# The second key's squared distance made on ScalarE, token by token, in place of a subtraction on Pool

## The chip, the cores and the metric

The kernel runs on one core of a Trainium2 chip. The metric is the time of one execution in microseconds on the device. A core has TensorE (matmuls; its weight loads are a line of their own in the profile), VectorE, ScalarE, Pool and the SyncE queue that issues DMAs. Each runs its own list of instructions in order, and they wait for one another by counting semaphores.

## The reference

One inference step of a decoder trunk of two layers, for 256 prompt tokens and 32 sample tokens (288 columns in all). Each layer is a mixer followed by a PEER channel mixer, which is where the change lies:

```python
def block(hb):
    q = (hb @ wq).reshape(T, PEER_HEADS, 2, PEER_DK // 2)
    s = jnp.einsum('thpc,hpkc->thpk', q, keys)
    v1, i1 = lax.top_k(s[:, :, 0], PEER_TOPK)
    v2, i2 = lax.top_k(s[:, :, 1], PEER_TOPK)
    comb = (v1[..., :, None] + v2[..., None, :]).reshape(T, PEER_HEADS, PEER_TOPK * PEER_TOPK)
    vals, sel = lax.top_k(comb, PEER_TOPK)
    e1 = jnp.take_along_axis(i1, sel // PEER_TOPK, axis=-1)
    e2 = jnp.take_along_axis(i2, sel % PEER_TOPK, axis=-1)
    eid = e1 * N_KEYS + e2
    gate = jax.nn.softmax(vals, axis=-1)
    act = jax.nn.gelu(jnp.einsum('thkd,td->thk', u[eid], hb), approximate=False)
    w = (gate * act).astype(hb.dtype)
    return jnp.einsum('thk,thkd->td', w, v[eid])
```

Each token has 8 heads with 16 picks each, so 128 picks, and each pick is a pair of keys (e1, e2) out of 128 x 128 experts.

## The kernel before

All 128 x 128 experts are computed for all tokens. In stage `u` of a layer TensorE multiplies the tokens with all of `peer_u`, and ScalarE writes the Gelu of it (L517) to `gates`, one column of 128 second keys for each first key and token. In stage `v` the weighted `gates` are multiplied with `peer_v`. The weights from Gelu to weighted `gates` are made in between, in the **gate loop**, which the change edits: for each token TensorE multiplies a 128 x 128 one-hot of the first key, scaled by the softmax gate, with a 128 x 128 one-hot of the second key, and the product (first key by second key) is multiplied into `gates`.

The gate loop has 12 iterations (`T // TOKENS`, 24 tokens each), and each iteration has six groups of four tokens (index `g`). The tile `choice` holds, with one row for each pick and one column for each token, the first key, the second key and the gate. It is filled by `turn_picks` on VectorE at the end of stage `u`. In each group:

- Pool (L367) writes into `apart` the distance of every second key from the picked one: `iota` (0 to 127 along the row) less the key, for four tokens in one instruction of 128x512.
- ScalarE squares `apart` (L528), and after its own semaphore makes 1 - square, cut off at 0, into `seconds` (L531, a Relu): this is the second one-hot.
- VectorE makes the first one-hots with four instructions of 128x128 (`firsts`, L1090).
- TensorE multiplies the two, token by token (L1409; a product of float32 is two matmuls in the profile), into PSUM.
- VectorE multiplies the 128x512 product into `gates` (`apply`, L1096). Its order is firsts of group 0, then for each group the firsts of it and the apply of the group before, and the last apply at the end of the iteration.

`apart` and `seconds` hold two groups, `onehot` eight tokens, PSUM two groups; `onehot_free`, `gate_free` and `second_ready` count them. Pool may write `apart` once the Relu two groups before is through.

In the first layer the gate loop carries the conditioning of the second layer as well. An iteration begins on TensorE with 16 matmuls of `condition` (L1212). ScalarE copies the result out in two halves (`next_row`, L470, after the Relu of groups 0 and 2), TensorE transposes each half after groups 1 and 3 (`turn`, L1239), and ScalarE adds the bias to the transposed columns (`next_column`, L477, two instructions each, after the Relu of groups 2 and 4).

Pool's list has, besides, the spill of x ahead of the gate loop and its reload, which waits for the first expert output of stage `v`.

Of the kernel before, what the change touches and what calls it, by code (L numbers as in the profile page):

```python
# [24 lines left out]
F32 = mybir.dt.float32  # L25
F32R = mybir.dt.float32r
U32 = mybir.dt.uint32
ALU = mybir.AluOpType
ACT = mybir.ActivationFunctionType
AX = mybir.AxisListType  # L30

P = 128
# [5 lines left out]
T = T_PROMPT + T_SAMPLE  # L38
# [63 lines left out]
def trunk(nc, t):  # L102

    with ExitStack() as ctx:
# [3 lines left out]
        def sem(name):  # L108
            return ctx.enter_context(nc.semaphore(name))
# [151 lines left out]
        exped, picks_ready = sem("exped"), sem("picks_ready")  # L261
        first_ready, second_ready = sem("first_ready"), sem("second_ready")
        onehot_free = sem("onehot_free")
        apart_ready, apart_squared = sem("apart_ready"), sem("apart_squared")
        gate_free = sem("gate_free")
        gelu_ready, topk_done, choice_ready, w_ready = sem("gelu_ready"), sem("topk_done"), sem("choice_ready"), sem("w_ready")
        w_high, w_low = sem("w_high"), sem("w_low")
# [74 lines left out]
        @block.gpsimd  # L342
        def _(pool):
            pool.dma_start(cs[:], t["c"]).then_inc(c_landed, 16)
            pool.dma_start(x, t["x"]).then_inc(x_landed, 16)
            for dst, src in ((ones[:], t["ones"]), (ident[:], t["ident"]), (iota[:], t["iota"]),
                             (ada_b[:], t["ada_b"]), (norm_g[:], t["norm_g"]), (small[:, 32:64], t["gains"])):
                pool.dma_start(dst, src).then_inc(const_landed, 16)
            for dst, src in ((cos_t, t["cos"]), (sin_t, t["sin"]), (swap, t["swap"]), (q_decay, t["q_decay"]),
                             (att_decay, t["att_decay"]), (att_decay_s[0:T_SAMPLE], t["att_decay_s"]),  # L350
                             (key_decay, t["key_decay"]), (seq_mask[0:T_SAMPLE], t["seq_mask"]),
                             (ret_state, t["state_ret"]), (conv_zs[:, :, :, 0:2], t["state_conv"])):
                pool.dma_start(dst, src).then_inc(ret_tables, 16)

            def peer(l):
                pool.wait_ge(mixer_done, l + 1)
                pool.dma_start(keys, t["peer_keys"][l]).then_inc(keys_landed, 16)
                pool.wait_ge(x_ready, 2 * l + 1)
                pool.dma_start(x_spill, x).then_inc(x_spilled, 16)

                pool.wait_ge(choice_ready, l + 1)
                pool.wait_ge(gelu_ready, EXP * (l + 1))
                with pool.Fori(0, T // TOKENS) as i:
                    for g in range(TOKENS // 4):
                        n = i * (TOKENS // 4) + (T // 4 * l + g)
                        pool.wait_ge(second_ready, n + 1)
                        pool.tensor_tensor(apart[:, g % 2], iota[:, None, :].broadcast_to([P, 4, P]),  # L367
                                           choice[:, 1, bass.ds(i * TOKENS + 4 * g, 4)][:, :, None].broadcast_to([P, 4, P]),
                                           ALU.subtract).then_inc(apart_ready, 1)
                pool.wait_ge(half_done, 2 * (SPLIT[f"v{l}"] + KC + 1))  # L370
                pool.dma_start(x, x_spill).then_inc(x_back, 16)


            pool.wait_ge(state_ready, 1)
            pool.dma_start(t["ret_p"], ret_s2).then_inc(state_stored, 16)
            pool.dma_start(t["ret_s"], ret_state).then_inc(state_stored, 16)
            pool.dma_start(t["conv_p"], conv_tail).then_inc(state_stored, 16)
            pool.dma_start(t["conv_s"], conv_tails).then_inc(state_stored, 16)
            peer(0)
            pool.wait_ge(half_done, 2 * (SPLIT["v0"] + EXP))  # L380
            for dst, src in ((restart, t["restart"]), (lev_mask, t["lev_mask"]), (lev_masks[0:T_SAMPLE], t["lev_masks"]),
                             (h_seq_mask[0:T_SAMPLE], t["seq_mask"]), (bounds, t["bounds"])):
                pool.dma_start(dst, src).then_inc(hg_tables, 16)

            def load_state(head, slot):
                pool.dma_start(s_in[:, slot:slot + 1], t["state_hgrn"][:, bass.ds(of_head(head, 1, 0), 1)]).then_inc(s_landed[slot], 16)

            def store_state(head, slot):
                pool.wait_ge(s_updated, of_head(head, 1, 1))
                pool.dma_start(t["hg_s"][:, bass.ds(of_head(head, 1, 0), 1)], s_out[:, slot:slot + 1]).then_inc(s_stored[slot], 16)  # L390
            for j in range(2):
                load_state((0, j), j)
            with pool.Fori(0, HG_HEADS // 2 - 1) as pair:
                for j in range(2):
                    store_state((pair, j), j)
                    pool.wait_ge(s_stored[j], pair * 16 + 16)
                    load_state((pair + 1, j), j)
            for j in range(2):
                store_state((HG_HEADS // 2 - 1, j), j)
            for j in range(2):  # L400
                pool.wait_ge(s_stored[j], 16 * (HG_HEADS // 2))
            pool.wait_ge(state_ready, 2)
            pool.dma_start(t["hg_p"], h_out).then_inc(state_stored, 16)
            peer(1)
            for half in range(2):
                chunks = slice(4 * half, 4 * half + 4)
                pool.wait_ge(y_ready, half + 1)
                pool.dma_start(t["y"][:, chunks], h[:, chunks]).then_inc(out_done, 16)
            pool.wait_ge(out_done, 32)
            pool.wait_ge(state_stored, 16 * 5)  # L410
            pool.wait_ge(x_spilled, 32)
# [3 lines left out]
        def _(act):  # L415
# [93 lines left out]
            def peer(l):  # L509
                norm(2 * l + 1)  # L510
                high_input(3 * l + 3)
                act.wait_ge(state_stored, 64 if l == 0 else 80)
                copy_out(f"wq{l}", query, ACT.Copy, (0, WQ // 4))
                act.wait_ge(x_spilled, 16 * (l + 1))

                def expert_in(i, s):
                    act.activation(gates[:, bass.ds(i * 4 + s, 1), :], ps[:, s % 2:s % 2 + 1, 0:T], ACT.Gelu).then_inc(gelu_ready, 1)  # L517
                read_out(f"u{l}", expert_in, groups=(0, topk_row // 4))
                act.wait_ge(topk_done, l + 1)
                act.activation(rstd[:], rstd[:], ACT.Exp).then_inc(exped, 1)  # L520
                read_out(f"u{l}", expert_in, groups=(topk_row // 4, EXP // 4))
                if l == 0:
                    act.sem_inc(second_ready, 2)
                with act.Fori(0, T // TOKENS) as i:
                    for g in range(TOKENS // 4):
                        n = i * (TOKENS // 4) + (T // 4 * l + g)
                        act.wait_ge(apart_ready, n + 1)
                        act.activation(apart[:, g % 2], apart[:, g % 2].bitcast(F32), ACT.Square).then_inc(apart_squared, 1)  # L528
                        act.wait_ge(apart_squared, n + 1)
                        act.wait_ge(onehot_free, i * TOKENS + (T * l + 4 * g + 4))  # L530
                        act.activation(seconds[:, g % 2], apart[:, g % 2].bitcast(F32), ACT.Relu, bias=1.0, scale=-1.0).then_inc(second_ready, 1)  # L531
                        if l == 0:
                            if g in (2, 4):
                                next_column(i + 12, g // 2 - 1, i * 4)
                            if g in (0, 2):
                                next_row(i + 12, g // 2)
                if l == 0:
                    high(SPLIT["v0"], FIRST["v0"] // 4, 0)

                def weight_high(e, slot):  # L540
                    act.activation(hs[:, 0, bass.ds(slot, 1), :], gates[:, bass.ds(e, 1), :], ACT.Copy).then_inc(w_high, 1)  # L541

                act.wait_ge(w_ready, (T // 4) * (l + 1))
                weight_high(0, 0)

                def expert_out(i, s):
                    split_high(f"v{l}", i, s)
                    if not (isinstance(i, int) and 4 * i + s == EXP - 1):
                        act.wait_ge(half_done, i * 8 + 2 * (SPLIT[f"v{l}"] + s))
                        weight_high(i * 4 + (s + 1), (s + 1) % 2)  # L550
                section(act, f"v{l}", expert_out)
# [83 lines left out]
        def _(dve):  # L635
# [15 lines left out]
            def released():  # L651

                dve.wait_ge(glue_free, taken.at())
# [414 lines left out]
            def turn_picks(l):  # L1068
# [6 lines left out]
                    ins = dve.transpose(choice[:, q, T_PROMPT:T], pick_of[2][:, q, :])  # L1075
                link(ins)
                released()
                dve.sem_inc(choice_ready, 1)

            def weigh(l):  # L1080
# [479 lines left out]
```

## Time and profile before

| | |
|---|---|
| median of 3 runs | 2921.69 us (2921.49 to 2928.01) |
| span of the profiled execution | 2932.5 us |
| TensorE busy | 2684.2 us (92%) |
| VectorE busy | 1793.5 us (61%) |
| ScalarE busy | 1351.1 us (46%) |
| Pool busy | 181.9 us (6%) |

The profile is one execution on the chip, and its times run from the first to the last instruction. A busy time is an average over stages with different limits, so each stage is read by itself. The granted clock is the share of full speed that TensorE's clock has in a stretch: 1.0 is 2.4 GHz and 0.5 is 1.2 GHz. In a timeline a row may merge several instructions of one line; the bracket behind it says how long the engine stood idle before and what it waited for.

### The profile page before, as it was taken

What the parts mean: (1) busy time and instruction counts of PE and PEld (TensorE: products, weight loads), DVE (VectorE), ACT (ScalarE), POOL (GpSimd) and SP (SyncE); (2) the same over time, 40 slices, a digit from 0 to 9 for tenths busy, and PEclk for the clock granted to TensorE, in tenths of its full rate; (3) what the DMA queues carried; (4) which work ended last, traced back from release to release, by engine and by line L of the source; (5) the groups of instructions that cost most, each with busy time, mean ns of one, the idle gap of its engine ahead of it and who ended that gap; (6) DMA issues with size and microseconds to landing.
All of it is one profiled execution on the core that took longest, in us unless ns stands there. A gap on an engine that the chain in (4) does not pass through costs nothing.

```text
span 2932.5 us, 55686 instructions
## 1 busy us (share of the span) xinstructions
PE 2684.2 (92%) x17972; PEld 2441.2 (83%) x17972; DVE 1793.5 (61%) x4076; ACT 1351.1 (46%) x2491; POOL 181.9 (6%) x200
## 2 busy tenths in 40 slices
PE   7997899999989899999979796999999866999997
PEld 3962799999955579999979685899999855999996
DVE  2424568884466755555554877589854599555554
ACT  2501345556543445555545323355556544455553
POOL 1000000000022310000000000000000144000000
PEclk8987899999998989999989788899999978999998
DMA  6544444545533335555534112345445300555552
GB/s 231 165 130 161 132 137 158 168 148 163 162 124 100 100 127 182 164 165 164 165 120 162 37 57 102 122 151 161 154 158 165 122 0 0 167 165 165 165 165 86
DMA packets 108380, 401.03 MB, mean 137 GB/s; under 512 B 12352, under 2 KB 12496, under 8 KB 107168
## 3 DMA queue, kind: packets, MB, share of 16 engines
q1 hardware_dynamic: 103104, 375.44, 39.7%
q0 software_dynamic: 5216, 24.87, 2.3%
q8 instruction: 29, 0.48, 0.1%
q14 instruction: 31, 0.25, 0.0%
HBM read 389.60 MB, written 10.65 MB: 136 GB/s over the span
## 4 chain that ended last, share of the span: by engine, by line
PE 81%; DVE 12%; issue 3%; ACT 2%; DMA 1%; DVEq 1%; ACTq 0%; POOL 0%; SPq 0%; POOLq 0%
PE ps L1184 21%; PE ps L1186 21%; PE ps L1185 21%; PE ps L1212 6%; PE ps L1409 4%; DVE onehot L1090 2%; DVE spl L660 1%; PE ps L1329 1%; PE ps L1345 1%; DVE big L1096 1%; PE ps L1358 1%; DMA raw<-in_ada_w 1%; PE ps L1248 1%; DVE big L1041 1%; DVE big L1036 1%
## 5 line engine op out<-in xcount | busy, mean ns | idle before, releaser
L1184 PE MATMUL ps<-hs,spl 128*128 128x288 f32 x4960 | 1481.8, 299 | 75.9 <-DVE hs L712 46.0
L1185 PE MATMUL ps<-hs,spl 128*128 128x288 f32 x4960 | 1473.0, 297 | 0.0
L1186 PE MATMUL ps<-hs,spl 128*128 128x288 f32 x4960 | 1470.5, 296 | 0.0
L660 DVE TENSOR_TENSOR spl<-raw,spl 128x512 fp32r<-128x512 f32 x1240 | 844.4, 692 | 844.9 <-ACT spl L422 842.6
L422 ACT ACTIVATE spl<-raw 128x512 fp32r<-128x512 f32 x1240 | 774.4, 631 | 628.6 <-PE ps L1186 628.2
L1184 PEld LDWEIGHTS ps<-hs,spl 128*128 128x128 f32 x4960 | 940.1, 190 | 89.5 <-issue 58.2
L1186 PEld LDWEIGHTS ps<-hs,spl 128*128 128x128 f32 x4960 | 943.0, 190 | 0.0
L1185 PEld LDWEIGHTS ps<-hs,spl 128*128 128x128 f32 x4960 | 941.7, 190 | 0.0
L1409 PE MATMUL ps<-hs,onehot 128*128 128x128 f32 x1152 | 222.7, 346 | 81.0 <-DVE onehot L1090 56.5
L1409 PEld LDWEIGHTS ps<-hs,onehot 128*128 128x128 f32 x1152 | 185.0, 239 | 121.3 <-issue 56.8
L1090 DVE TENSOR_SCALAR onehot<-iota,choice 128x128 f32<-128x128 f32 x576 | 239.2, 480 | 5.5 <-PEq L1398 4.4
L367 POOL TENSOR_TENSOR hs<-iota,choice 128x512 fp32r<-128x512 f32 x144 | 152.3, 1058 | 1245.7 <-ACT big L517 1002.5
L1212 PE MATMUL ps<-raw,cs 128*10 128x512 f32 x384 | 184.5, 636 | 13.6 <-ACT cs L554 6.7
L517 ACT ACTIVATE big<-ps 128x288 f32 (+1 forms) x256 | 105.6, 412 | 177.9 <-PE ps L1186 177.2
L1212 PEld LDWEIGHTS ps<-raw,cs 128*10 128x10 f32 x384 | 34.7, 96 | 147.2 <-issue 128.5
L1096 DVE TENSOR_TENSOR big<-big,ps 128x512 f32 x144 | 98.0, 681 | 86.7 <-PE ps L1409 85.7
L531 ACT ACTIVATE hs<-hs 128x512 fp32r<-128x512 f32 x144 | 91.0, 632 | 86.6 <-PE ps L1409 78.0
L1123 DVE TENSOR_TENSOR hs<-big,hs 128x288 fp32r<-128x288 f32 x256 | 115.8, 452 | 0.6 <-ACT hs L541 0.6
L541 ACT ACTIVATE hs<-big 128x288 fp32r (+1 forms) x256 | 109.9, 429 | 5.5 <-DVEq L1104 5.5
L517 ACT ACT_TABLE_LOAD x62 | 79.5, 1283 | 63.1 <-PE ps L1186 63.1
L528 ACT ACTIVATE hs<-hs 128x512 fp32r<-128x512 f32 x144 | 88.7, 616 | 3.2 <-POOL hs L367 3.1
L484 ACT ACTIVATE big<-ps 128x288 f32 (+1 forms) x92 | 37.9, 412 | 95.8 <-PE ps L1186 95.7
(222 smaller groups left out, 1292.3 us busy)
## 6 DMA issues: line engine op xcount, KB each, us to landing
raw<-in_peer_u SPq DMA_DIRECT2D x256, 512.0 KB, 3.4
raw<-in_peer_v SPq DMA_DIRECT2D x256, 512.0 KB, 3.4
raw<-in_ada_w SPq DMA_DIRECT2D x96, 512.0 KB, 4.3
raw<-in_peer_wq SPq DMA_DIRECT2D x32, 512.0 KB, 3.3
raw<-in_hg_w_in SPq DMA_DIRECT2D x32, 512.0 KB, 3.4
raw<-in_ab_w_in SPq DMA_DIRECT2D x28, 512.0 KB, 3.4
raw<-in_ab_w_out SPq DMA_DIRECT2D x8, 512.0 KB, 3.9
big<-in_state_hgrn POOLq DMA_DIRECT2D x8, 512.0 KB, 3.9
```

What stands on the lines that cost most here:

```text
L367: pool.tensor_tensor(apart[:, g % 2], iota[:, None, :].broadcast_to([P, 4, P]), choice[:, 1, bass.ds(i * TOKENS + 4 * g, 4)][:, :, None].b ...
L422: act.activation(spl[:, slot % 2, 0, cols], raw[:, slot, cols], ACT.Copy).then_inc(high_ready, 1)
L517: act.activation(gates[:, bass.ds(i * 4 + s, 1), :], ps[:, s % 2:s % 2 + 1, 0:T], ACT.Gelu).then_inc(gelu_ready, 1)
L660: dve.tensor_tensor(spl[:, slot % 2, 1, cols], raw[:, slot, cols], spl[:, slot % 2, 0, cols].bitcast(F32), ALU.subtract).then_inc(low_read ...
L1090: dve.tensor_scalar(onehot[:, (4 * g + j) % 8, :], iota[:], choice[:, 0, bass.ds(tok, 1)], choice[:, 2, bass.ds(tok, 1)], ALU.is_equal, AL ...
L1096: dve.tensor_tensor(w, w, ps[:, 6 + g % 2, :].rearrange("p (j e) -> p e j", j=4), ALU.mult).then_inc(gate_free, 1)
L1123: dve.tensor_tensor(hs[:, 1, slot, :], gates[:, bass.ds(e, 1), :].rearrange("p a t -> p (a t)"), hs[:, 0, slot, :].bitcast(F32), ALU.subtr ...
L1184: pe.matmul(out, spl[:, slot, 0, cols], high, start=start, stop=False, skip_group_check=True)
L1185: pe.matmul(out, spl[:, slot, 0, cols], low, start=False, stop=False, skip_group_check=True)
L1186: return pe.matmul(out, spl[:, slot, 1, cols], high, start=False, stop=stop, skip_group_check=True)
L1212: ins = pe.matmul(out, cs[:, k, :], raw[:, k // 2, ROWS * (k % 2):ROWS * (k % 2) + ROWS], start=k == 0, stop=k == KC - 1)
L1409: pe.matmul(ps[:, 6 + g % 2, j * P:j * P + P], onehot[:, (4 * g + j) % 8, :], seconds[:, g % 2, j, :].bitcast(F32), start=True, stop=True) ...
```

## The change

The subtraction on Pool and its semaphore are gone. VectorE negates the second key in `choice` once, at the end of `turn_picks`. ScalarE makes the square by itself: four instructions of 128x128 for a group, each with `iota` as input and the token's column of the negated key as bias, and the last one of the four raises the semaphore that the Relu waits for. ScalarE now waits for `choice_ready` ahead of the loop, and for the Relu two groups before (its own) in place of Pool.

```diff
-                pool.wait_ge(choice_ready, l + 1)
-                pool.wait_ge(gelu_ready, EXP * (l + 1))
-                with pool.Fori(0, T // TOKENS) as i:
-                    for g in range(TOKENS // 4):
-                        n = i * (TOKENS // 4) + (T // 4 * l + g)
-                        pool.wait_ge(second_ready, n + 1)
-                        pool.tensor_tensor(apart[:, g % 2], iota[:, None, :].broadcast_to([P, 4, P]),
-                                           choice[:, 1, bass.ds(i * TOKENS + 4 * g, 4)][:, :, None].broadcast_to([P, 4, P]),
-                                           ALU.subtract).then_inc(apart_ready, 1)
...
+                act.wait_ge(choice_ready, l + 1)
                 with act.Fori(0, T // TOKENS) as i:
                     for g in range(TOKENS // 4):
                         n = i * (TOKENS // 4) + (T // 4 * l + g)
-                        act.wait_ge(apart_ready, n + 1)
-                        act.activation(apart[:, g % 2], apart[:, g % 2].bitcast(F32), ACT.Square).then_inc(apart_squared, 1)
+                        act.wait_ge(second_ready, n + 1)
+                        for j in range(4):
+                            ins = act.activation(apart[:, g % 2, j], iota[:], ACT.Square, bias=choice[:, 1, bass.ds(i * TOKENS + (4 * g + j), 1)])
+                        ins.then_inc(apart_squared, 1)
                         act.wait_ge(apart_squared, n + 1)
...
                 link(ins)
                 released()
+                link(dve.tensor_scalar(choice[:, 1, :], choice[:, 1, :], -1.0, None, ALU.mult))
                 dve.sem_inc(choice_ready, 1)
```

## Rows read from the trace of the kernel before

**Rows 1.** Stretch table: stretch, length, busy us (count), granted clock, DMA share, GB/s
```profile
824.40:1065.00 240.60, 212.78 (x864) 121.43 (x864) 159.06 (x360) 103.94 (x218) 75.42 (x72) 0.87 0.32 105
2325.90:2492.40 166.50, 112.92 (x576) 96.39 (x576) 161.24 (x360) 83.44 (x144) 76.92 (x72) 0.79 0.00 1
```

**Rows 2.** Source view of two lines: ns min/median/max, first and last start
```profile
L1090 DVE TENSOR_SCALAR onehot<-iota,choice x576: 332/340/1223, 824.5 to 2490.7; 128x128 f32<-128x128 f32 x192
L367 POOL TENSOR_TENSOR hs<-iota,choice x144: 1030/1041/1183, 824.5 to 2485.9; 128x512 fp32r<-128x512 f32 x144
```

**Rows 3.** Timeline of VectorE, both layers: start us, us, instructions [idle before]
```profile
2341.35 2.97 DVE L1090 TENSOR_SCALAR onehot<-iota,choice 128x128 f32<-128x128 f32 x8
...
925.69 2.14 DVE L1090 TENSOR_SCALAR onehot<-iota,choice 128x128 f32<-128x128 f32 x8
...
2488.32 1.11 DVE L1090 TENSOR_SCALAR onehot<-iota,choice 128x128 f32<-128x128 f32 x4
2489.34 0.68 DVE L1096 TENSOR_TENSOR big<-big,ps 128x512 f32 x1
2489.94 1.11 DVE L1090 TENSOR_SCALAR onehot<-iota,choice 128x128 f32<-128x128 f32 x4
```

**Rows 4.** Timeline of TensorE: groups at full and half clock, and a bubble
```profile
2488.79 1.18 PE L1409 MATMUL ps<-hs,onehot 128*128 128x128 f32 x8 [0.44 <-DVE onehot L1090]
...
842.58 2.02 PE L1409 MATMUL ps<-hs,onehot 128*128 128x128 f32 x8 [0.30 <-ACT hs L531]
...
2342.67 2.56 PE L1409 MATMUL ps<-hs,onehot 128*128 128x128 f32 x11 [2.10 <-DVE onehot L1090]
```

**Rows 5.** Timeline of ScalarE, start of the second layer's loop
```profile
2327.74 0.63 ACT L531 ACTIVATE hs<-hs 128x512 fp32r<-128x512 f32 x1
2328.27 0.61 ACT L528 ACTIVATE hs<-hs 128x512 fp32r<-128x512 f32 x1
2329.00 0.63 ACT L531 ACTIVATE hs<-hs 128x512 fp32r<-128x512 f32 x1
```

**Rows 6.** Groups of ScalarE by form: busy us, mean ns of one | idle before
```profile
L528 ACT ACTIVATE hs<-hs 128x512 fp32r<-128x512 f32 x144 | 88.7, 616 | 3.2 <-POOL hs L367 3.1
...
L594 ACT ACTIVATE big<-big 128x1280 f32<-128x1280 f32 x8 | 10.1, 1257 | 0.7 <-DVE big L880 0.7
...
L457 ACT ACTIVATE mod<-ps,ada_b 128x10 f32<-128x10 f32 x48 | 9.0, 272 | 22.9 <-PE ps L1231 22.7
L470 ACT ACTIVATE rstd<-ps 10x256 f32<-10x256 f32 x24 | 8.8, 366 | 96.2 <-PE ps L1212 96.2
```

**Rows 7.** Timeline of ScalarE: four instructions in a row, each with a bias tile
```profile
34.26 0.75 ACT L457 ACTIVATE mod<-ps,ada_b 128x10 f32<-128x10 f32 x4 [0.34 <-PE ps L1231]
```

**Rows 8.** Timelines of ScalarE and VectorE: ends of the second layer's loop
```profile
2325.08 0.41 ACT L517 ACTIVATE big<-ps 128x288 f32<-128x288 f32 x1 [2.27 <-PE ps L1186]
...
2325.89 5.13 DVE L1090 TENSOR_SCALAR onehot<-iota,choice 128x128 f32<-128x128 f32 x8 [1.11 <-ACT big L517]
...
2488.39 0.63 ACT L531 ACTIVATE hs<-hs 128x512 fp32r<-128x512 f32 x1 [0.42 <-PE ps L1409]
```

**Rows 9.** Timelines of TensorE and ScalarE: one iteration of the first layer's loop
```profile
913.91 1.16 PE L1409 MATMUL ps<-hs,onehot 128*128 128x128 f32 x8 [0.64 <-ACT hs L531]
...
917.89 0.94 PE L1409 MATMUL ps<-hs,onehot 128*128 128x128 f32 x6 [0.67 <-ACT hs L531]
919.23 0.57 PE L1409 MATMUL ps<-hs,onehot 128*128 128x128 f32 x2 [0.40 <-DVE onehot L1090]
919.73 1.02 PE L1239 MATMUL ps<-ident,rstd 10*128 10x10 f32 x4
...
924.87 7.74 PE L1212 MATMUL ps<-raw,cs 128*10 128x512 f32 x16
...
915.84 0.48 ACT L477 ACTIVATE mod<-ps,ada_b 128x10 f32 x2 [0.72 <-PE ps L1239]
...
920.98 0.56 ACT L477 ACTIVATE mod<-ps,ada_b 128x10 f32 x2 [1.89 <-PE ps L1239]
```

## What was predicted, and from what

> **What bounds the kernel now.** The change touches two stretches only, the gate loops of the two layers, so the first view is the stretch table, cut at their ends [rows 1]: 240.60 us in the first layer, 166.50 us in the second, of a span of 2932.5 us. Each is 12 iterations of six groups of four tokens, so 20.05 and 13.88 us an iteration. In the second layer VectorE is busy for 161.24 of 166.50 us: it is the bound. In the first layer TensorE is busy for 212.78 of 240.60 us, because each iteration also holds 16 conditioning matmuls (7.74 us in [rows 9]).
>
> Then the source view of the two lines that meet [rows 2]. A one-hot on VectorE (L1090) has a median of 340 ns and a maximum of 1223 ns; a subtraction on Pool (L367) has 1041 ns. The timeline shows what stretches the one-hots [rows 3]: eight of them take 2.97 us where a Pool subtraction runs beside them (2341.35) and 2.14 us where Pool is idle (925.69). After the last subtraction (it starts at 2485.9 [rows 2]) a group of four takes 1.11 us, and VectorE goes round once in 1.62 us (2488.32 to 2489.94). So one subtraction costs VectorE about 0.83 us, most of its own 1.04 us, and a round of the second layer, 13.88 / 6 = 2.31 us, is about 0.7 us longer than VectorE needs alone. I take this as exclusion between the two engines.
>
> TensorE needs 1.18 us for the 8 matmuls of a group at a granted clock of 1.0 and 2.02 us at 0.5 [rows 4]; the stretches' means are 0.87 and 0.79 [rows 1]. ScalarE has slack now: 83.44 of 166.50 us busy.
>
> **What goes.** The 144 subtractions leave Pool, and with them a semaphore hop from ScalarE to Pool and back. Nothing else on Pool moves: its reload of x still sits behind the wait for the expert output stage. What VectorE gets back is about 0.83 us a group, 60 us in each layer, of which only what no other engine needs becomes time.
>
> **What comes on ScalarE.** One Square of 128x512 becomes four of 128x128, each with a column of the choice tile as bias. Now a Square starts 0.53 us after the Relu before it, and the Relu 0.73 us after its Square [rows 5]: a round takes at least 1.27 us. For the small Square there is no row, so I bound it. Its length: 616 ns at 512 columns and 1257 at 1280 make 0.835 ns a column [rows 6], so 128 columns without a bias tile last 616 - 384 x 0.835 = 295 ns. The bias tile: L470 (256 columns, no bias tile) takes 366 ns, L457 (10 columns, with one) 272 ns [rows 6]; by columns the second should be 205 ns shorter and is 94 shorter, so the tile adds 0.11 us, and a small Square lasts 0.40 us. Its distance to the next: 0.53 - 384 x 0.000835 = 0.21 us if the tile costs nothing (lower bound); four L457 take 0.75 us [rows 7], so (0.75 - 0.27) / 3 = 0.16 us apart, and with 118 columns more 0.26; 0.32 if the tile's 0.11 is paid in full on top of 0.21; 0.40 if neighbours don't overlap (upper bound). I take 0.30, between the two middle values, as L457 reads PSUM and the Square reads SBUF. The address arithmetic of each Square runs on ScalarE's sequencer; I count it as hidden, and if it isn't, the upper bound is the case.
>
> The Trainium skill prices the same thing: "ScalarE: Activation LUTs", section "What ACT_TABLE_LOAD costs", says that a [128,1] pointer operand adds some 93 ns, that such an ACTIVATE takes about 280 ns + 0.833 ns a column, and that neighbours overlap by 93 ns. By that, as an estimate, a Square takes 387 ns at a distance of 294 ns, and the sum below would move by some 2 us.
>
> From the first Square to the Relu: 3 x 0.30 + 0.40 + 0.12 (0.73 less the Square's 0.616) = 1.42 us in place of 0.73. A round of ScalarE is then 1.42 + 0.53 = 1.95 us, above VectorE's free 1.62: **ScalarE becomes the bound of the second layer**.
>
> **Second layer.** The last Gelu starts at 2325.08 and lasts 0.41 [rows 8]. The Squares begin at 2325.5, the first Relu at 2326.9, the 72nd 71 x 1.95 = 138.5 us later, at 2465.4; before, it started at 2488.39 [rows 8]. That is 23 us less with TensorE at full clock. At half clock TensorE needs 2.02 us a group, and between iterations it stands still: VectorE applies the sixth group before it makes the next one-hots. This bubble is 2.10 us now [rows 4]; without Pool I reckon 0.7 (the apply of 2489.34 in [rows 3]) + 0.35 (first one-hot) + 0.1 = 1.15. So 6 x 2.02 + 1.15 = 13.3 us an iteration, and 12 x 0.58 = 7 us less than before is the poorest end. Groups of 8 matmuls every 1.62 us ran at full clock at the end of this loop [rows 4], and 1.95 us is not far from that: I take -22.
>
> **First layer.** Here three Squares stand in TensorE's way, for ScalarE is held by conditioning work in between. In an iteration [rows 9] the second group waits for its Relu (913.91), the fourth again (917.89) after L477 had waited for the first transposes (915.84), and the sixth's Square comes behind the second L477 (920.98). Each of the three becomes 0.69 us longer, so 2.1 us. Against that, the fourth group no longer waits for VectorE in its midst: its 8 matmuls would end 1.07 us after 917.89, the transposes behind them start at 919.73, so 0.8 us comes back. At the same clock an iteration is thus up to 1.3 us longer, and less where stretched one-hots, and not this chain, set its end now. If the clock falls one group earlier than now, the fourth group takes 2.02 in place of 1.1 us ahead of the chain: 2.3 us longer. I take 1.0 us, 12 us for the layer; ends 0 and +28.
>
> **Small edits.** The negation is one VectorE instruction on 128x288 (between 0.34 at 128 columns [rows 2] and 0.68 at 512 [rows 3]) and its wait, 0.5 us a layer. It lies in the 1.11 us that VectorE waits for the last Gelu in the second layer [rows 8], and beside the first conditioning matmuls in the first layer. If that cover were gone: 1 us in all. ScalarE's new wait for the choice holds up only the Squares behind it, and by then the choice is there. Both: 0, at most +1.
>
> **The sum**: -22 + 12 = -10 us. The profiled execution is given by its span, 2932.5 us; the runs have a median of 2921.69 (2921.49 to 2928.01), and 10 us scaled by their ratio stays 10. So 2911.7 us.
>
> **Rivals.**
> (a) *The clock pays it back.* TensorE's gaps grow in the first layer, and what falls to half clock makes the chain longer. Evidence: both loops already run at 0.87 and 0.79, not at 1.0. Price: -8 in the second layer, +28 in the first, so +20: 2942. It decides once most iterations of the first layer fall to half clock before the fourth group. The Trainium skill speaks for it: "TensorE: Matmul & The Clock Gate", section "HAM oscillation", says that idle stretches between bursts of matmuls bring the throttle back and that each burst then starts slow. The rows of half-clock groups agree that it happens here; whether more often after the change no row shows.
> (b) *Small Squares don't overlap* (0.40 apart): first Square to Relu 1.72, a round 2.25. Second layer 71 x 0.30 = 21 us worse, so about -1; first layer 3 x 0.3 x 12 = 11 worse, +23: slower by 22, 2944. Each 0.01 us of distance is worth some 3 us; the balance tips at 0.33. Against it: neighbours do overlap in [rows 5] and [rows 7].
> (c) *The bias tile is free* (0.21 apart, 0.30 long): a round 1.05 + 0.53 = 1.58, so VectorE's 1.62 bounds the second layer: 71 x 1.62 = 115 us, -46 at full clock, with bubbles and some half clock -33. First layer 0.3 less on each of three Squares, 0. About -33: 2889. Against it: the 0.11 us of [rows 6].
> (d) *The one-hots aren't stretched by Pool* but by something that stays: VectorE keeps its 13.88 us in the second layer, and in the first the fourth group still waits for it in part, so more than 12 us are paid there: +15, 2937. [Rows 3] speak against it.
>
> **Chances.** Forecast 0.45, (a) 0.22, (b) 0.15, (c) 0.13, (d) 0.05. The forecast's own range is 2897 to 2925. The range runs from (c) at its better half to (a): 2886 to 2943. A measurement here can tell about 0.3% (8.8 us) from no change. Faster by more: three quarters of the forecast and all of (c), 0.47. Within: the rest of the forecast and the milder part of (a) and (b), 0.27. Slower: 0.26.
>
> **What would show it.** L1090 at a mean near 340 ns in both layers; small Squares some 0.40 us long and 0.30 apart; the second layer's loop near 144 us with ScalarE busy for almost all of it and TensorE waiting for the Relu, no longer for one-hots; the first layer's loop near 252 us with longer waits of the second, fourth and sixth group for their Relus. Wrong if one-hots stay stretched, if Squares stand 0.35 us apart, or if the granted clock of either loop moves by more than 0.05.

## The result, and the profile after

The changed kernel takes 2929.99 us (median of 20 runs) where the one before took 2924.59 us beside it: a ratio of 1.0021, with a 95% interval of 1.0012 to 1.0029. It is slower by 0.2%, some 6 us: less than the 0.3% that the prediction called no change, but its interval is clear of zero, on the other side than the forecast of -10 us. Behind this small number stand two large ones of opposite sign. The stretch table of the changed kernel, cut at the ends of the two loops (stretch, length, busy us and count of TensorE, its weight loads, VectorE, ScalarE and Pool, granted clock, DMA share, GB/s):

```profile
816.10:1089.00 272.90, 233.55 (x864) 135.98 (x864) 123.16 (x360) 149.53 (x433) 0.00 (x0) 0.75 0.29 92
2351.80:2490.60 138.80, 88.50 (x576) 75.79 (x576) 120.05 (x360) 129.17 (x359) 0.00 (x0) 0.95 0.00 2
```

These answer to [rows 1], but they run from the first one-hot of a loop to the start of its last apply. By the same two marks the kernel before, in its profiled execution, has

```profile
824.50:1064.80 240.30, 212.74 (x864) 121.37 (x864) 158.86 (x359) 103.94 (x218) 75.40 (x72) 0.87 0.32 105
2325.90:2491.70 165.80, 112.92 (x576) 96.39 (x576) 160.56 (x359) 83.44 (x144) 76.92 (x72) 0.79 0.00 1
```

The second loop won 27.0 us (165.8 to 138.8), the first lost 32.6 (240.3 to 272.9): +5.6 net. Between the two stretches little moved (1261.1 us before, 1262.8 after). The profiled executions themselves differ by -1.2 us (2932.5 and 2931.3), because the first loop began 8.4 us earlier after the change (816.1 in place of 824.5). The part up to there runs the same instructions in both kernels but for the negation, and in the executions profiled below the loop begins anywhere from 814.0 to 821.5. I put that down to chance, which no run shows, and so compare loops and medians, not spans.

The changed instructions, by line (first the source view, ns min/median/max, then ScalarE's groups by form):

```profile
L1085 DVE TENSOR_SCALAR onehot<-iota,choice x576: 331/341/347, 816.1 to 2488.1; 128x128 f32<-128x128 f32 x192
...
L521 ACT ACTIVATE hs<-iota,choice 128x128 fp32r<-128x128 f32 x576 | 182.0, 386 | 0.0
L525 ACT ACTIVATE hs<-hs 128x512 fp32r<-128x512 f32 x144 | 90.7, 630 | 16.6
```

The one-hots' maximum fell from 1223 ns [rows 2] to 347 ns, and a small Square lasts 386 ns. ScalarE's timeline at the start of the second loop gives the round:

```profile
2351.34 1.28 ACT L521 ACTIVATE hs<-iota,choice 128x128 fp32r<-128x128 f32 x4
2352.73 0.63 ACT L525 ACTIVATE hs<-hs 128x512 fp32r<-128x512 f32 x1
2353.27 1.26 ACT L521 ACTIVATE hs<-iota,choice 128x128 fp32r<-128x128 f32 x4
2354.64 0.63 ACT L525 ACTIVATE hs<-hs 128x512 fp32r<-128x512 f32 x1
```

From one Relu to the next are 1.91 us: four Squares in 1.26, so (1.26 - 0.386) / 3 = 0.29 apart, and 1.38 from the first of them to the Relu. 72 rounds are 137.5 us, and the loop took 138.8. All 71 distances between its Relus are 1.91 or 1.92 us. ScalarE bounds the second layer, as forecast. TensorE's bubble between two iterations of this loop, 2.10 us in [rows 4], is now 1.27 us, where the prediction reckoned 1.15:

```profile
2365.41 4.60 PE L1404 MATMUL ps<-hs,onehot 128*128 128x128 f32 x24 [1.27 <-DVE onehot L1085]
```

One iteration of the first loop on TensorE, with the conditioning ahead of it (L1207), answers to [rows 9]:

```profile
928.95 8.54 PE L1207 MATMUL ps<-raw,cs 128*10 128x512 f32 x16
937.42 1.16 PE L1404 MATMUL ps<-hs,onehot 128*128 128x128 f32 x8
939.87 1.16 PE L1404 MATMUL ps<-hs,onehot 128*128 128x128 f32 x8 [1.29 <-ACT hs L525]
940.95 0.61 PE L1234 MATMUL ps<-ident,rstd 10*128 10x10 f32 x4
941.78 1.67 PE L1404 MATMUL ps<-hs,onehot 128*128 128x128 f32 x8 [0.21 <-ACT hs L525]
944.49 2.08 PE L1404 MATMUL ps<-hs,onehot 128*128 128x128 f32 x8 [1.04 <-ACT hs L525]
946.50 1.02 PE L1234 MATMUL ps<-ident,rstd 10*128 10x10 f32 x4
947.45 2.08 PE L1404 MATMUL ps<-hs,onehot 128*128 128x128 f32 x8
950.23 2.08 PE L1404 MATMUL ps<-hs,onehot 128*128 128x128 f32 x8 [0.70 <-ACT hs L525]
```

The reader is to see two things. TensorE now waits for Relus alone: ahead of the second, fourth and sixth group, and for 0.21 us ahead of the third. And a group takes 1.16 us in the first half and 2.08 in the second: the clock falls to its lower level in the third group, one group earlier than [rows 9] had it, stays there for the rest of the iteration, and the conditioning behind it starts slow too. Not every iteration is like this one: the third group is slowed in eight of the twelve and the fourth takes 2.08 us in nine, while in the other three the clock falls only behind the fourth. The conditioning takes 7.9 to 8.9 us in eleven of the twelve, where 7.74 was the figure in [rows 9]. The mean clock of this loop fell from 0.87 to 0.75; that of the second loop rose from 0.79 to 0.95.

### The profile page after: what moved, and what is told of

Same layout as the page of the kernel before. It is cut to its first block, busy times and chain, and to the rows that moved or that the text cites. A ratio compares the mean times of both kernels' runs of the same rounds, so it can differ in the third digit from the quotient of the medians.

```text
span 2931.3 us, 56190 instructions
## 1 busy us (share of the span) xinstructions
PE 2676.1 (91%) x17972; PEld 2435.0 (83%) x17972; DVE 1717.4 (59%) x4078; ACT 1440.7 (49%) x2923; POOL 29.4 (1%) x56
## 4 chain that ended last, share of the span: by engine, by line
PE 82%; DVE 9%; ACT 5%; issue 2%; DMA 1%; ACTq 1%; DVEq 0%; POOL 0%; SPq 0%; POOLq 0%
PE ps L1179 21%; PE ps L1181 21%; PE ps L1180 21%; PE ps L1207 6%; PE ps L1404 4%; ACT hs L521 3%; DVE spl L654 1%; PE ps L1324 1%; ACT hs L525 1%; PE ps L1340 1%; PE ps L1353 1%; DMA raw<-in_ada_w 1%; PE ps L1243 1%; DVE big L1035 1%; DVE big L1030 1%
## 5 line engine op out<-in xcount | busy, mean ns | idle before, releaser
L1404 PE MATMUL ps<-hs,onehot 128*128 128x128 f32 x1152 | 207.9, 337 | 90.2 <-ACT hs L525 65.2
L1404 PEld LDWEIGHTS ps<-hs,onehot 128*128 128x128 f32 x1152 | 177.2, 235 | 123.9 <-ACT hs L525 113.0
L1207 PE MATMUL ps<-raw,cs 128*10 128x512 f32 x384 | 189.2, 650 | 11.9 <-ACT cs L548 6.6
L521 ACT ACTIVATE hs<-iota,choice 128x128 fp32r<-128x128 f32 x576 | 182.0, 386 | 0.0
L1085 DVE TENSOR_SCALAR onehot<-iota,choice 128x128 f32<-128x128 f32 x576 | 157.9, 341 | 4.9 <-PEq L1393 4.1
L1207 PEld LDWEIGHTS ps<-raw,cs 128*10 128x10 f32 x384 | 35.3, 97 | 149.6 <-issue 130.4
L525 ACT ACTIVATE hs<-hs 128x512 fp32r<-128x512 f32 x144 | 90.7, 630 | 16.6
L461 ACT ACTIVATE rstd<-ps 10x256 f32<-10x256 f32 x24 | 8.7, 364 | 100.0 <-PE ps L1207 100.0
```

What stands on the lines that cost most here:

```text
L521: ins = act.activation(apart[:, g % 2, j], iota[:], ACT.Square, bias=choice[:, 1, bass.ds(i * TOKENS + (4 * g + j), 1)])
L1085: dve.tensor_scalar(onehot[:, (4 * g + j) % 8, :], iota[:], choice[:, 0, bass.ds(tok, 1)], choice[:, 2, bass.ds(tok, 1)], ALU.is_equal, AL ...
L1207: ins = pe.matmul(out, cs[:, k, :], raw[:, k // 2, ROWS * (k % 2):ROWS * (k % 2) + ROWS], start=k == 0, stop=k == KC - 1)
L1404: pe.matmul(ps[:, 6 + g % 2, j * P:j * P + P], onehot[:, (4 * g + j) % 8, :], seconds[:, g % 2, j, :].bitcast(F32), start=True, stop=True) ...
```

## The experiments

**Each layer alone.** My theory after the result: the layers pull opposite ways, and each effect stays in its own loop. Two kernels give one loop the new code and leave Pool the other (there Pool adds the negated key, where it subtracted the key before). The edit on ScalarE, with 0 for the layer that keeps Pool:

```diff
+                        if l == 0:
+                            act.wait_ge(apart_ready, i * (TOKENS // 4) + (g + 1))
+                            act.activation(apart[:, g % 2], apart[:, g % 2].bitcast(F32), ACT.Square).then_inc(apart_squared, 1)
+                        else:
                             act.wait_ge(second_ready, n + 1)
                             for j in range(4):
```

> The first layer's gate loop keeps Pool's part (an addition of the negated key in place of the subtraction), only the second layer's loop makes the squares from the key column on ScalarE. Theory (the two layers pull opposite ways: the second gains because VectorE is released, the first loses because ScalarE's longer squares stand in TensorE's chain): the first loop stays near 240 us as before, the second near 140, so about 26 us (0.9%) less than the kernel before. Rival (the traces of before and after differ by chance in the first layer, and the gain of the second is given back elsewhere, in the stage behind it): within 0.3% of before.

Measured: 2894.25 us, ratio 0.9914 (0.9888 to 0.9939). The loops: 237.4 and 138.8 us.

> The reverse: only the first layer's loop has the new squares, the second keeps Pool. Theory: the first loop takes about 273 us in place of 240, the second stays near 166, so 30 to 35 us (1.1%) more than before. Rival (a difference by chance): within 0.3% of before.

Measured: 2953.59 us, ratio 1.0110 (1.0090 to 1.0129). The loops: 270.5 and 165.6 us. Both rivals fall. The effects add up, and the change in the second layer alone is faster by 0.9%.

**Is it the clock or the chain?** In the first loop the chain of Squares and Relus is longer, and the clock is lower. To tell them apart I added work: matmuls on two constant tiles into a PSUM bank that is unused there, placed where TensorE waits. They can't shorten a chain; they can only keep TensorE busy.

```diff
                         if l == 0 and g in (1, 3):
                             turn(i + 12, g // 2)
+                        if l == 0:
+                            for _ in range((4, 2, 4, 2, 4, 0)[g]):
+                                pe.matmul(ps[:, 2, 0:P], ident[:], iota[:], start=True, stop=True)
```

> The changed kernel with matmuls added in the first layer's gate loop, whose product is never read: 4, 2, 4, 2 and 4 of 128 columns in float32 behind the first to fifth group of each iteration, where TensorE waits for a Relu. They add 16 x 0.27 = 4.3 us of TensorE work at full clock to an iteration that has about that much idle time. Theory A (most of the first layer's loss is the granted clock, which falls in those gaps): the clock of the loop rises from about 0.77 to above 0.9, groups take 1.16 us, the conditioning 7.0 us in place of 8 to 8.9, an iteration about 20 us in place of 22.7, the kernel 25 to 33 us less than the changed one. Theory B (the loss is the longer chain of squares and Relus alone): the added work gains nothing, 2930 us or more, since the chain is as long as before.

Measured: 2889.97 us, ratio 0.9898 (0.9879 to 0.9917), 40 us under the changed kernel with more work to do. The first loop and an iteration of it on TensorE:

```profile
814.00:1048.50 234.50, 220.26 (x1248) 141.54 (x1248) 123.09 (x359) 149.56 (x433) 0.00 (x0) 1.00 0.34 107
...
911.61 7.03 PE L1207 MATMUL ps<-raw,cs 128*10 128x512 f32 x16
918.57 1.16 PE L1404 MATMUL ps<-hs,onehot 128*128 128x128 f32 x8
919.57 1.06 PE L1410 MATMUL ps<-iota,ident 128*128 128x128 f32 x8
921.02 1.16 PE L1404 MATMUL ps<-hs,onehot 128*128 128x128 f32 x8 [0.40 <-ACT hs L525]
```

The clock is 1.00 throughout, the conditioning takes 7.03 us, each group 1.16 or less, and the loop 234.5 us in place of 272.9. Theory A holds, B falls: 38.4 us of the changed first loop are the clock.

Half the dose, and the same dose in another place, as controls (2, 1, 2, 1, 2 and 0; then all 16 behind the sixth group, where there is no gap):

> The run with filled gaps at half the dose: 2, 1, 2, 1 and 2 products in each iteration. Clock theory: the clock lies between 0.75 and 1.0 and the first loop between 234.5 and 272.9 us, with iterations of both kinds. Rival (the added work helps in some other way, in proportion): 254 us with every iteration alike.

Measured: 2896.27 us, ratio 0.9908 (0.9881 to 0.9934). The first loop and the starts of two iterations:

```profile
821.50:1057.50 236.00, 204.51 (x1056) 126.33 (x1056) 123.22 (x359) 149.56 (x433) 0.00 (x0) 0.98 0.33 107
...
927.12 1.16 PE L1404 MATMUL ps<-hs,onehot 128*128 128x128 f32 x8
...
946.65 1.16 PE L1404 MATMUL ps<-hs,onehot 128*128 128x128 f32 x8
```

It took 236.0 us at a clock of 0.98, near the full dose and not halfway, and the conditioning takes 7.03 or 7.04 us in every iteration. So the gain is not in proportion to the added work. An iteration in which the clock doesn't fall lasts 19.53 us (927.12 to 946.65), and with the full dose 19.53 too, so the added matmuls don't lengthen it; the few in which it falls last about 20.0.

> A control of the run with added matmuls: the same 16 products of 128 columns in each iteration of the first loop, but all behind the sixth group, right ahead of the conditioning matmuls, where TensorE has no gap. Theory (what helps is that the gaps are filled): the clock in the groups falls as in the changed kernel, an iteration is as long as there (22.7 us) plus 4.3 us or more of added work less what a full clock at the conditioning gives back (about 1.3), so the first loop near 309 us and the kernel near 2966. Rival (any added work in the iteration holds the clock): near the 234.5 us of the filled gaps, 2890 to 2900.

Measured: 2973.86 us, ratio 1.0173 (1.0149 to 1.0197). The loop took 311.8 us at a clock of 0.79, and the groups run much as in the changed kernel:

```profile
814.40:1126.20 311.80, 270.05 (x1218) 187.61 (x1219) 123.17 (x359) 149.52 (x433) 0.00 (x0) 0.79 0.26 81
...
925.79 1.16 PE L1404 MATMUL ps<-hs,onehot 128*128 128x128 f32 x8
928.24 1.16 PE L1404 MATMUL ps<-hs,onehot 128*128 128x128 f32 x8 [1.29 <-ACT hs L525]
...
935.61 2.08 PE L1404 MATMUL ps<-hs,onehot 128*128 128x128 f32 x8
938.39 2.07 PE L1404 MATMUL ps<-hs,onehot 128*128 128x128 f32 x8 [0.70 <-ACT hs L525]
940.25 5.22 PE L1410 MATMUL ps<-iota,ident 128*128 128x128 f32 x32
```

It is the filling of the gaps that holds the clock, not the added work as such.

**What the chain costs by itself.** The kernel before, with the clock held up in its first loop in the same way (2, 2, 4, 2, 3 and 0):

> The kernel before the change with matmuls added whose product is never read: 2, 2, 4, 2 and 3 of 128 columns behind the first to fifth group of each iteration of the first layer's gate loop. With the clock held up in both kernels the difference of their first loops is the price of the longer chain alone; the changed kernel with the clock held took 234.5 us there. Theory (the chain costs some 0.4 us an iteration net, the clock all the rest): clock near 1.0, first loop 228 to 233 us. Rival 1 (the chain as I added it up costs 1.3 us an iteration): 219 us. Rival 2 (VectorE, held up by Pool, is the bound here too once the clock is full): 234 us or more, and the added work gains nothing.

Measured: 2915.18 us, ratio 0.9967 (0.9952 to 0.9982). The first loop:

```profile
819.00:1046.50 227.50, 215.96 (x1176) 135.85 (x1176) 162.69 (x359) 103.70 (x218) 75.56 (x72) 1.00 0.34 111
```

It took 227.5 us at a clock of 1.00, just under the band of the theory; both rivals fall. The kernel before thus paid 240.3 - 227.5 = 12.8 us to the clock in this loop, and the longer chain costs 234.5 - 227.5 = 7.0 us, 0.6 an iteration. In this kernel the added matmuls may themselves delay a group here and there, which no run rules out, so I count each part as uncertain by a few us.

**Squares ahead of the conditioning.** If the three Squares that stand in TensorE's way are what opens the gaps, moving them out should close them:

```diff
+                    squares(i, 0)
                     for g in range(TOKENS // 4):
...
                         act.activation(seconds[:, g % 2], apart[:, g % 2].bitcast(F32), ACT.Relu, bias=1.0, scale=-1.0).then_inc(second_ready, 1)
+                        if g + 1 < TOKENS // 4:
+                            squares(i, g + 1)
                         if l == 0:
                             if g in (2, 4):
                                 next_column(i + 12, g // 2 - 1, i * 4)
```

Here `squares` is the wait and the four activations of the change, unaltered.

> The changed kernel with one thing moved: ScalarE makes the four squares of the next group right behind the Relu of this one, ahead of the conditioning columns and rows, so that they run while TensorE does the conditioning or the transposes. Theory A and B agree on the direction: three squares of 1.38 us leave the chain. B (chain alone): 3 x 1.38 = 4.1 us less an iteration at most, so the first loop near 225 to 235 us. A (clock as well): the gaps shrink too and the clock rises above 0.85. The second layer stays near 140 us. The kernel 2885 to 2900 us, under both the one before and the changed one. Rival (the order of ScalarE doesn't matter, TensorE is the bound of the first loop): 2930 us.

Measured: 2868.92 us, ratio 0.9825 (0.9806 to 0.9844). The first loop, and one of its iterations:

```profile
814.70:1026.60 211.90, 185.67 (x864) 104.51 (x864) 120.92 (x360) 141.08 (x433) 0.00 (x0) 0.96 0.37 119
...
911.69 2.21 PE L1410 MATMUL ps<-hs,onehot 128*128 128x128 f32 x16
913.83 0.61 PE L1240 MATMUL ps<-ident,rstd 10*128 10x10 f32 x4
914.66 1.16 PE L1410 MATMUL ps<-hs,onehot 128*128 128x128 f32 x8 [0.22 <-ACT hs L529]
916.91 1.16 PE L1410 MATMUL ps<-hs,onehot 128*128 128x128 f32 x8 [1.09 <-ACT hs L529]
```

The first two groups follow one another without a gap, since the second group's Squares are made while TensorE does the conditioning. The loop is shorter than I expected (211.9 us against 225 to 235), and so is the kernel (2868.9 against 2885 to 2900); the loop is 61 us shorter than the changed kernel's. With gaps still open behind the third and fifth group, the added matmuls were tried here too:

> The kernel with the squares moved ahead of the conditioning work, and added matmuls that nobody reads behind the second, third, fourth and fifth group (1, 4, 1 and 3) of each iteration of the first loop. There the clock was 0.96 without them and the loop 211.9 us. Clock theory: clock 1.0, all iterations at the 17.2 us of an undisturbed one, so 206 to 209 us and 3 to 6 us less than without them (2863 to 2866). Rival (added work costs as much as the last 4% of the clock give back): 2868 us or more.

Measured: 2862.12 us, ratio 0.9780 (0.9764 to 0.9797), and a first loop of 206.4 us at a clock of 1.00. This is the fastest version found, 2.2% under the kernel before. With the clock held in both, moving the Squares is thus worth 234.5 - 206.4 = 28.1 us in this loop; the other 33 of the 61 us are the clock, which stays up in most of the iterations once the Squares are moved.

**What the second layer gained from.** Pool gets its work back, without a reader:

```diff
+                        pool.wait_ge(second_ready, n + 1)
+                        pool.tensor_tensor(unread[:, g % 2], iota[:, None, :].broadcast_to([P, 4, P]),
+                                           choice[:, 1, bass.ds(i * TOKENS + 4 * g, 4)][:, :, None].broadcast_to([P, 4, P]),
+                                           ALU.add).then_inc(beside, 1)
+                        pool.wait_ge(beside, n + 1)
```

> The changed kernel with Pool doing its 144 additions of 128x512 beside it, behind the Relu two groups before, into a part of the work tile that nobody reads, each waiting for the one before. ScalarE makes the squares by itself as in the changed kernel. Theory (Pool's instruction and VectorE's one-hots exclude each other, and that alone set the second layer's pace): one-hots go back to a mean near 480 ns, the second loop from 138.8 to 160 us or more. Rival (what was won in the second layer is the semaphore hop over Pool): one-hots stretched or not, the second loop stays near 139 us.

Measured: 2941.23 us, ratio 1.0057 (1.0039 to 1.0076). The second loop, its one-hots, and VectorE and Pool side by side:

```profile
2353.50:2502.90 149.40, 99.81 (x576) 85.42 (x576) 148.53 (x359) 129.27 (x359) 75.91 (x72) 0.89 0.00 1
...
L1096 DVE TENSOR_SCALAR onehot<-iota,choice 128x128 f32<-128x128 f32 x288 | 109.1, 442 | 0.8 <-ACT big L519 0.8
...
2419.79 1.10 DVE L1096 TENSOR_SCALAR onehot<-iota,choice 128x128 f32<-128x128 f32 x4
2421.45 1.84 DVE L1096 TENSOR_SCALAR onehot<-iota,choice 128x128 f32<-128x128 f32 x4
...
2421.56 1.13 POOL L368 TENSOR_TENSOR hs<-iota,choice 128x512 fp32r<-128x512 f32 x1 [1.78 <-ACT hs L536]
```

Pool's instructions alone stretch the one-hots from 340 to 442 ns on average, and VectorE is the bound again (148.53 of 149.40 us). The rival falls. But the size misses: 149.4 us, not 160, and 442 ns, not 480. Exclusion by itself accounts for 10.6 of the 27 us in this order of work. For the rest I asked the clock of the kernel before, with two added products behind every group of its second loop (its first left alone):

> The kernel before with two added products of 128 columns that nobody reads behind every group of the second layer's loop (3.2 us an iteration at full clock; the first layer is left alone). Adding Pool's instructions to the changed kernel brought back 10.6 of the 27 us that the second loop had lost; this asks what the other 16 were. Theory 1 (the granted clock, 0.79 there before and 0.95 after the change): the clock rises to 0.95 or more and the second loop falls from 165.8 to about 150 us. Theory 2 (Pool's subtraction itself, as it falls beside the one-hots in this order of work): the clock rises and the loop stays within 3 us of 165.8, with one-hots at a mean near 475 ns.

Measured: 2914.87 us, ratio 0.9971 (0.9958 to 0.9983). The second loop:

```profile
2317.80:2475.20 157.40, 120.12 (x863) 105.38 (x864) 156.52 (x359) 83.23 (x144) 76.88 (x72) 0.99 0.00 1
```

The clock rose to 0.99 and the loop took 157.4 us: 8.4 less, between the two theories. One-hots were still at a mean of 469 ns. So of the 27 us some 8 go with the clock. The other 18.6 are VectorE's: with the clock held it stands idle for 0.9 us of this loop, and for 0.9 us of the one with Pool's unread additions, so its busy time sets the pace in both. That is 156.52 us here and 148.53 there: 8.0 us more, because its one-hots are stretched further in the old order of work (469 ns against 442). The last 10.6 come when Pool falls silent. By then ScalarE, and not VectorE, is the bound.

## Why the prediction was wrong

**The price of ScalarE's part was right.** A Square of 0.40 us at a distance of 0.30 measured 0.386 at 0.29; first Square to Relu 1.42, measured 1.38; a round 1.95, measured 1.91. Rivals (b), no overlap, and (c), a free bias tile, are out. The Trainium skill's figures ("ScalarE: Activation LUTs", section "What ACT_TABLE_LOAD costs") come out, as an estimate, as 387 ns at a distance of 294; the trace agrees within 3 ns.

**VectorE's release was right in kind and too large in size**: the one-hots' mean fell to 341 ns, rival (d) is out, and the run with Pool's instructions put back shows the exclusion. But the forecast of 60 us for VectorE in each layer, 0.83 a group, measured 40.5 in the second (160.56 to 120.05 us busy) and 35.7 in the first (158.86 to 123.16). Nothing in the sum hung on it, as VectorE bounds neither loop after the change.

**The second layer**: -22 forecast, -27.0 measured. The walk was right, and its terms were off by little. From the start of the last Gelu to the 72nd Relu it had 140.3 us; measured are 137.7, because a round is 1.91 us and not 1.95. The last apply starts 2.0 us behind the last Relu, where it was 3.3 before: 1.4 us that the sum didn't count. The 1 us taken off for half clock wasn't paid: the mean clock rose to 0.95, and where it still falls for a spell, the rounds stay at 1.91 us. One sign came only in part: TensorE was to wait for the Relu and no longer for one-hots, and the profile puts 24.6 us of its waits in this loop to one-hots and 26.4 to the Relu.

**The small edits** cost nothing that shows: the negation lasts 309 ns, and VectorE still waits 0.8 us for the last Gelu in the second layer.

**The step that failed is the first layer's sum, "I take 1.0 us".** That made 12 us for the layer, and the bounds were 0 and +28; the loop lost 32.6, above the upper one. At a held clock the chain costs 0.6 us an iteration, below my 1.0 and within the "up to 1.3" of the walk. The rest, 32.6 - 7.0 = 25.6 us, is the clock, which costs 38.4 us in this loop after the change and 12.8 before. I had counted a fall one group earlier as the bad end, 2.3 us an iteration, and taken a middle value for no other reason than that it is one. The trace shows the fourth group at half clock in nine of twelve iterations, and one more item that the bad end lacked: the conditioning behind the groups starts at the lower level and lasts 7.9 to 8.9 us where it took 7.0 to 7.8 before.

**Rival (a) had the mechanism, and its form was wrong.** Its condition, most iterations at half clock before the fourth group, came true, and so did the prediction's own sign of being wrong, a clock that moves by more than 0.05: it did in both loops. But I tied both loops to one clock story and let the second layer lose as well (-8). There the clock rose: TensorE's idle time went from 27.6 to 39.4 us in the first loop, and from 52.9 to 50.3 in the second, where the bubble between iterations fell from 2.10 to about 1.3 us. That filled gaps raise the clock of the second loop too, the last run above shows; that the shorter bubble did it after the change is likely, and not shown. The Trainium skill ("TensorE: Matmul & The Clock Gate", section "HAM oscillation") says that idle stretches between bursts of matmuls bring the throttle back. In the first loop the filled gaps, the half dose and the misplaced dose agree, at 1.00, 0.98 and 0.79. The page's case is waits for DMA; here the gaps are waits of 0.2 to 1.6 us for ScalarE.

**What was luck.** The measured time lies inside the prediction's range (2886 to 2943), but only because -27.0 and +32.6 nearly cancel; the first layer by itself left its bounds.

## What to carry to other kernels

When work moves onto an engine's chain ahead of TensorE, price the gaps that it opens by what they do to the granted clock and not only by their length: here a chain longer by 0.6 us an iteration cost 2.7. Ask it of each stage separately: the same edit lowered the clock in one loop and raised it in the other. And where an engine in order serves two masters, look first for what can be made ahead of a wait: moving the Squares before the conditioning work turned +0.2% into -1.8%.

## What the runs showed of the hardware

Matmuls that nobody reads made a loop faster: with 16 products of 128 columns more in each iteration, the changed first loop fell from 272.9 to 234.5 us, and half of them did nearly as well (236.0). In this loop the clock had two levels: groups take 1.16 us or 2.08, and some lie between because it changes in their midst. The idle share alone doesn't tell the clock: after the change TensorE stands idle for 36% of the second loop at a clock of 0.95, and for 14% of the first at 0.75; no run here shows what makes the difference. A Pool instruction of 128x512 in float32 and VectorE's one-hots of 128x128 don't run side by side: four one-hots take 1.10 us alone and 1.84 beside the Pool instruction of 2421.56, and in the traces a one-hot that a Pool instruction stretches ends 0.08 us behind it. VectorE's apply, which reads PSUM, isn't slowed: it lasted 677 ns on average in the second loop with Pool's unread additions and 683 without.
